# Differential attention in another order: scores one map at a time, the map turned two units later, the heads scaled by ScalarE

## What is computed

```python
def diff_attention(q, k, v, lam):
    ...
    def block(qblk):
        s = jnp.einsum('bqhcd,bkhcd->bhcqk', qblk, k).astype(jnp.float32) * scale
        pr = jax.nn.softmax(s, axis=-1)
        a = (pr[:, :, 0] - lam * pr[:, :, 1]).astype(v.dtype)
        return jnp.einsum('bhqk,bkhe->bqhe', a, v)
```

## Time and profile before

| | |
|---|---|
| time, median of 3 runs | 1784.78 us (1784.57 to 1785.18) |
| the profiled execution's own time | 1786.67 us |
| span of its trace | 1784.5 us |
| mean granted TensorE clock | 0.969 |
| busy share of the span | PE 87%, DVE 35%, ACT 14%, POOL 14% |
| attention: first scores to last product | 279.44 to 369.37 us |

### The profile page before, as it was taken

How to read it: one execution, slowest core, us unless ns; L and a number is a source line. 1 busy time by engine, 2 the same in 40 slices (tenths; PEclk the granted TensorE clock), 3 DMA queues, 4 the chain that set the end, 5 groups by cost and what they waited for, 6 DMA issues and landing times.

```text
span 1784.5 us, 19903 instructions
## 1 busy us (share of the span) xinstructions
PE 1550.3 (87%) x6788; PEld 715.9 (40%) x6788; DVE 616.7 (35%) x1194; ACT 249.2 (14%) x497; POOL 247.2 (14%) x376
## 2 busy tenths in 40 slices
PE   4999897789999999888884799999899999898881
PEld 2445444545433333333332344545433333333330
DVE  2499645743622222122123320233622222212224
ACT  2110023621100000000002111011100000000001
POOL 0024020000112111111110001000121121121110
PEclk9899998999999999999997899999999999999996
DMA  9754233041699999999997654252899999999995
GB/s 345 262 175 174 97 140 154 25 154 45 233 415 418 419 419 420 420 420 420 421 418 288 222 196 142 95 236 75 310 418 420 417 418 419 420 420 420 419 421 225
DMA packets 118640, 534.15 MB, mean 299 GB/s; under 512 B 18185, under 2 KB 19010, under 8 KB 68138
## 3 DMA queue, kind: packets, MB, share of 16 engines
q1 hardware_dynamic: 96016, 493.46, 68.9%
q0 software_dynamic: 12032, 21.08, 3.2%
q10 hardware_dynamic: 10522, 18.64, 3.0%
HBM read 522.55 MB, written 27.33 MB: 308 GB/s over the span
## 4 chain that ended last, share of the span: by engine, by line
PE 38%; SPq 19%; DMA 15%; DVE 4%; issue 3%; ACT 2%; ACTq 0%; POOLq 0%; DVEq 0%
SPq L497 18%; PE psum_pair_B L1775 12%; DMA scratch<-w_up 8%; PE psum_pair_C L1797 7%; PE psum_pair_B L1666 4%; PE psum_pair_A L1666 4%; DMA weight_ring<-w_up 3%; PE psum_pair_C L1713 3%; PE psum_pair_D L1713 3%; DMA scratch<-modulation_rows 1%; DMA weight_ring<-w_ada 1%; PE psum_pair_C L1607 1%; PE psum_pair_D L1784 1%; PE psum_pair_D L1706 1%; DVE scratch L1351 1%
## 5 line engine op out<-in xcount | busy, mean ns | idle before, releaser
L1775 PE MATMUL psum_pair_B<-weight_ring,gates_by_token 128*64 128x512 f32 x1408 | 313.5, 594 | 25.4 <-DMA weight_ring<-w_up 21.8
L1775 PE MATMUL psum_pair_B<-scratch,gates_by_token 128*64 128x512 f32 x896 | 199.3, 593 | 11.4 <-DMA scratch<-w_up 11.4
L1351 DVE TENSOR_TENSOR scratch<-psum_pair_B,scratch 128x256 f32<-128x256 f32 x72 | 30.6, 424 | 507.5 <-ACT scratch L884 507.5
L1775 PEld LDWEIGHTS psum_pair_B<-weight_ring,gates_by_token 128*64 128x64 f32 x1408 | 112.5, 137 | 218.8 <-issue 194.2
L1797 PE MATMUL psum_pair_C<-weight_ring,scratch 128*64 128x512 f32 x704 | 160.8, 597 | 25.0 <-issue 22.6
L692 POOL DMA_INDIRECT expert_rows<-scratch,scatter_rows x72 | 73.4, 1019 | 717.7 <-DVE scratch L1363 717.7
L1666 PE MATMUL psum_pair_A<-scratch,weight_ring 128*128 128x128 f32 (+1 forms) x512 | 146.4, 444 | 4.4 <-DVE scratch L1402 2.8
L884 ACT ACTIVATE scratch<-psum_pair_B 128x256 f32<-128x256 f32 x72 | 27.6, 383 | 841.9 <-PE psum_pair_B L1775 841.9
L1666 PE MATMUL psum_pair_B<-scratch,weight_ring 128*128 128x128 f32 (+1 forms) x512 | 142.2, 436 | 0.0
L1775 PEld LDWEIGHTS psum_pair_B<-scratch,gates_by_token 128*64 128x64 f32 x896 | 74.7, 137 | 131.5 <-issue 120.2
L1445 DVE SCALAR_TENSOR_TENSOR weight_ring<-weight_ring,params 128x655 f32<-128x655 f32 x120 | 117.1, 976 | 5.0 <-DVE gates_by_token L1093 0.9
(11 more groups left out here) (357 smaller groups left out, 1478.2 us busy)
## 6 DMA issues: line engine op xcount, KB each, us to landing
weight_ring<-w_gate SPq DMA_DIRECT2D x88, 1024.0 KB, 27.2
weight_ring<-w_up SPq DMA_DIRECT2D x88, 1024.0 KB, 28.2
weight_ring<-w_down SPq DMA_DIRECT2D x88, 1024.0 KB, 28.1
weight_ring<-w_ada SPq DMA_DIRECT2D x24, 2048.0 KB, 8.7
scratch<-w_up SPq DMA_DIRECT2D x40, 1024.0 KB, 27.9
scratch<-w_down SPq DMA_DIRECT2D x40, 1024.0 KB, 27.6
scratch<-w_gate SPq DMA_DIRECT2D x40, 1024.0 KB, 26.6
weight_ring<-w_in_e SPq DMA_DIRECT2D x5, 2048.0 KB, 14.5
```

The lines of the kernel that those rows point to most:

```text
L1351: tt(HID[par], PB[B_][:, 512 * par + 256:512 * par + 512], SIL[par], ALU.mult).then_inc(sig("hidden", l), 1)
L1775: ins = mm(PB[B_][CAP * q:CAP * (q + 1), 512 * par:512 * par + 512].rearrange("p (u n) -> p u n", u=2), XGT[par][:, at:at + CAP], w[:, :, ...
```

## The change

Scores and maxima are issued one map at a time: `scores(u, c)`, `maxima(u, c)`, `exps(u, c)`. TensorE now runs `scores(i, 0)`, `turn(i-2)`, `scores(i, 1)`, `values(i-2)`. VectorE runs `maxima(i, 0)`, `mixed(i-1)`, `maxima(i, 1)`; its `heads_out` is gone. ScalarE runs `turned(i-2)`, `exps(i, 0)`, `head_squares(i-3)`, `heads_out(i-2)`, `exps(i, 1)`; `heads_out` is now an ACTIVATE with Copy and a scale by partition. Its loop has one more round, VectorE's one less. The allocation of PSUM pairs and the sizes are as before.

```diff
--- before.py
+++ after.py
@@ -975,15 +975,12 @@
             act.dma_start(out["new_cache_k"].rearrange("b l t h c d -> (b l t) (h c d)"), KC).then_inc(sig("outputs_stored"), 16)
             after(act, "v", 4)
             act.dma_start(out["new_cache_v"].rearrange("b l t h c -> (b l t) (h c)"), V[:, 4, :]).then_inc(sig("outputs_stored"), 16)
-            def exps(u):
+            def exps(u, c):
                 w = NS + PAST if UNITS[u][0] < 4 else NP
-                for c in range(2):
-                    take(act, "s", u, c)
-                    act.wait_ge(sig("max_ready"), 2 * u + c + 1)
-                    if u >= 2 and c == 0:
-                        take(act, "aT", u - 2)
-                    took(act.activation(PR[:, u % 2, c, 0:w], PB[uses[("s", u, c)][0]][:, 0:w], ACT.Exp, bias=snb[:, u % 2, c:c + 1],
-                                        scale=DH ** -0.5, accum_out=sl[:, u % 2, c:c + 1]), "s", u, c)
+                take(act, "s", u, c)
+                act.wait_ge(sig("max_ready"), 2 * u + c + 1)
+                took(act.activation(PR[:, u % 2, c, 0:w], PB[uses[("s", u, c)][0]][:, 0:w], ACT.Exp, bias=snb[:, u % 2, c:c + 1],
+                                    scale=DH ** -0.5, accum_out=sl[:, u % 2, c:c + 1]), "s", u, c)
 
             def turned(u):
                 w = NS + PAST if UNITS[u][0] < 4 else NP
@@ -992,6 +989,11 @@
                     take(act, "av", u - 2)
                 took(act.activation(AT[:, u % 2, 0:w], p[:, 0:w], ACT.Copy), "aT", u)
 
+            def heads_out(u):
+                t, h = UNITS[u]
+                p = take(act, "av", u)
+                took(act.activation(OR[:, t, h * 128:(h + 1) * 128], p[:, 0:128], ACT.Copy, scale=sr[:, u % 2, 0:1]), "av", u)
+
             def head_squares(u):
                 t, h = UNITS[u]
                 after(act, "av", u)
@@ -1000,13 +1002,17 @@
                 act.activation(SQJ[u % 2], OR[:, t, h * 128:(h + 1) * 128], ACT.Square, accum_out=oss[:, 4 * t + h:4 * t + h + 1]).then_inc(sig("head_squares"), 1)
 
             NU = len(UNITS)
-            for i in range(NU + 2):
+            for i in range(NU + 3):
+                if 2 <= i < NU + 2:
+                    turned(i - 2)
                 if i < NU:
-                    exps(i)
-                if 1 <= i <= NU:
-                    turned(i - 1)
-                if i >= 2:
-                    head_squares(i - 2)
+                    exps(i, 0)
+                if i >= 3:
+                    head_squares(i - 3)
+                if 2 <= i < NU + 2:
+                    heads_out(i - 2)
+                if i < NU:
+                    exps(i, 1)
                 if i == 8:
                     modulation_columns(0)
                 if i == 14:
@@ -1482,12 +1488,11 @@
             for name, j in [("q", 2), ("q", 3)] + [("k", j) for j in range(HC)]:
                 roped(name, j)
 
-            def maxima(u):
+            def maxima(u, c):
                 w = NS + PAST if UNITS[u][0] < 4 else NP
-                for c in range(2):
-                    p = take(dve, "s", u, c)
-                    link(dve.tensor_reduce(smx[:, u % 2, c:c + 1], p[:, 0:w], AX_X, ALU.max))
-                    ts(snb[:, u % 2, c:c + 1], smx[:, u % 2, c:c + 1], -DH ** -0.5, None, ALU.mult).then_inc(sig("max_ready"), 1)
+                p = take(dve, "s", u, c)
+                link(dve.tensor_reduce(smx[:, u % 2, c:c + 1], p[:, 0:w], AX_X, ALU.max))
+                ts(snb[:, u % 2, c:c + 1], smx[:, u % 2, c:c + 1], -DH ** -0.5, None, ALU.mult).then_inc(sig("max_ready"), 1)
 
             def mixed(u):
                 w = NS + PAST if UNITS[u][0] < 4 else NP
@@ -1499,19 +1504,14 @@
                 link(stt(sr[:, u % 2, 1:2], sl[:, u % 2, 0:1], lam_neg, sr[:, u % 2, 1:2], ALU.mult, ALU.mult))
                 stt(PR[:, u % 2, 0, 0:w], PR[:, u % 2, 1, 0:w], sr[:, u % 2, 1:2], PR[:, u % 2, 0, 0:w], ALU.mult, ALU.add).then_inc(sig("a_ready"), 1)
 
-            def heads_out(u):
-                t, h = UNITS[u]
-                p = take(dve, "av", u)
-                took(ts(OR[:, t, h * 128:(h + 1) * 128], p[:, 0:128], sr[:, u % 2, 0:1], None, ALU.mult), "av", u)
-
             NU = len(UNITS)
-            for i in range(NU + 2):
-                if 1 <= i <= NU:
+            for i in range(NU + 1):
+                if i < NU:
+                    maxima(i, 0)
+                if i >= 1:
                     mixed(i - 1)
                 if i < NU:
-                    maxima(i)
-                if i >= 2:
-                    heads_out(i - 2)
+                    maxima(i, 1)
                 if i == 18:
                     router_constant(0)
 
@@ -1915,19 +1915,16 @@
                 ins = pe.transpose(p[:, h * 128:(h + 1) * 128], kT[:, h, NS:], ident)
             filled(ins, "kout")
 
-            def scores(u):
+            def scores(u, c):
                 t, h = UNITS[u]
-                ps = [fill(pe, "s", u, c) for c in range(2)]
-                rows = [slice(DH * c, DH * (c + 1)) for c in range(2)]
-                q = [qT[rows[c], h, t * 128:(t + 1) * 128] for c in range(2)]
+                p = fill(pe, "s", u, c)
+                rows = slice(DH * c, DH * (c + 1))
+                q = qT[rows, h, t * 128:(t + 1) * 128]
                 if t < 4:
-                    for c in range(2):
-                        mm(ps[c][:, 0:NS], q[c], kT[rows[c], h, 0:NS], start=True, stop=True)
-                    for c in range(2):
-                        filled(mm(ps[c][:, NS:NS + PAST], q[c], kcT[rows[c], h, :], start=True, stop=True), "s", u, c)
+                    mm(p[:, 0:NS], q, kT[rows, h, 0:NS], start=True, stop=True)
+                    filled(mm(p[:, NS:NS + PAST], q, kcT[rows, h, :], start=True, stop=True), "s", u, c)
                 else:
-                    for c in range(2):
-                        filled(mm(ps[c][:, 0:NP], q[c], kT[rows[c], h, NS:], start=True, stop=True), "s", u, c)
+                    filled(mm(p[:, 0:NP], q, kT[rows, h, NS:], start=True, stop=True), "s", u, c)
 
             def turn(u):
                 p = fill(pe, "aT", u)
@@ -1952,9 +1949,11 @@
             NU = len(UNITS)
             for i in range(NU + 2):
                 if i < NU:
-                    scores(i)
-                if 1 <= i <= NU:
-                    turn(i - 1)
+                    scores(i, 0)
+                if i >= 2:
+                    turn(i - 2)
+                if i < NU:
+                    scores(i, 1)
                 if i >= 2:
                     values(i - 2)
             cat0 = lambda k: catU[:, k, :] if k < 4 else oT[:, k - 4, :]
```

## The result

The changed kernel takes **1843.93 us** (median of 4 runs, 1841.5 to 1845.0) against 1784.67 us for the kernel before in the same comparison (1782.33 to 1785.18, 4 runs): a ratio of **1.033**, 95% interval 1.0311 to 1.0349. It is slower by 59 us, where 7.5 us less were forecast, and the time lies far outside the range.

What follows compares the result with a forecast made beforehand. The attention was taken as bound by a chain of waits, 4.41 us per unit, with no engine full. Steady part -2.3, filling -4.6, emptying -0.9 and DMA issues +0.3 summed to -7.5: 1777.3 us, range 1774.3 to 1783.5.

Steps and rivals of the forecast that it cites:

- the filling: Attention's start, up to unit 4's scores: unit 1 waits only for exponential 0, clock stays up; -4.6 us.
- The third rival: Attention: clock falls and stays low as half the rows rest; 8.2 us per unit, 1798 to 1830 us; chance 0.10.
- the emptying: From unit 16's scores to the last product's end: 14.3 us instead of 15.2; -0.9 us, bounds -2 and +1.
- unit 4's start: Its scores start near 296.7; at 301.3, as before, if the clock falls and returns only at 296.36.
- VectorE and ScalarE stopped being the bound: Attention units: VectorE 3.3 to 3.4 us, ScalarE 2.8, below TensorE's 4.22, which takes over as the bound.
- The scaled head on ScalarE: Head scaling moved from VectorE to ScalarE: 0.3 us per unit, bounds 0.2 and 0.4.
- The round of 4.22 us: TensorE's time per attention unit: two maps at 1.22, transposes 0.57, products 1.21; bounds 4.08 and 4.56.
- the change of tiling: Step from a map's last score matmul to the next full-array matmul: 0.18 us, bounds 0.11 and 0.35.
- The first rival: TensorE empties fully at tiling switches: round 4.56 to 4.6 us, total about 1783 us; chance 0.13.
- The steady part: Twelve middle attention units, each 4.22 instead of 4.41 us: -2.3 us, bounds -4.0 and +1.8.
- The DMA issues of ScalarE: Behind i = 8 in ScalarE's queue, now followed by a turned map's copy with slack of about 1.2: +0.3 us.
- Faster at all?: Whole kernel: chance 0.70 of being faster, meaning below 1781.2 us; 0.19 the same, 0.11 slower.

Runs made afterwards that it cites:

- run 4: The changed kernel with four useless full-row matmuls behind unit 0's scores and two behind unit 1's; 1785.81 us, ratio 0.9982.
- run 10: As run 4, but the useless matmuls take 64 of the 128 rows; 1785.51 us, ratio 0.9998.
- run 1: The changed kernel with each map's score matmuls over all 128 rows, so other attention values; 1774.22 us, ratio 0.9926.
- run 11: The changed kernel with the other map's score matmuls beside each map's own, unread, only from unit 4 on; 1792.5 us, ratio 1.0039.
- run 9: The changed kernel with ten extra useless full-row matmuls once, ahead of unit 4's transposes; 1813.06 us, ratio 1.0146.
- run 3: The kernel before with only its scores issued apart, VectorE and ScalarE as before; 1847.11 us, ratio 1.0327.
- run 2: The changed kernel with both maps' scores issued by turns as before, VectorE and ScalarE as changed; 1828.82 us, ratio 1.0226.
- run 6: The changed kernel with queries zero-padded to 128 rows, values kept, one expert weight load moved behind the attention; 1775.96 us, ratio 0.9934.
- run 5: The changed kernel with the other map's score matmuls run beside each map's own in the other 64 rows, unread; 1783.86 us, ratio 0.9987.

## Why the prediction was wrong

**The cause.** Three things are shown. A wait of 3.3 us lets the clock fall (runs 4 and 10 fill the wait, and the fall is gone). Then the separated scores, over half the rows and at half speed, did not get it raised again in the changed kernel, while full rows did, in the same list (runs 1 and 11); a block of full rows did too (run 9). At the high clock the same list stays up (runs 4, 9, 10). That twice the speed means twice the work in a given time would explain this; it is argued, not shown. Before, both maps ran side by side over all rows, and the clock was back at unit 3. Not shown is the rule by which the chip decides. Four things that any such rule has to meet were not taken apart: run 3's two returns with half rows, its two falls without a long wait, run 2's long low stretch with full rows, and a first wait of about the same length that let the clock fall in runs 1 and 6 (2.28 us) and not in run 5 (2.24 us).

**The step that failed** is the filling, at "this supposes that the clock stays up". It rested on 1.1 us more of work before the wait and on a wait of 2.5 us instead of 4.19. The work was never there. Unit 0's maps still ran side by side, because nothing stands between `scores(0, 0)` and `scores(0, 1)` for i < 2:

```profile
279.76 0.66 PE L1924 MATMUL psum_pair_A<-scratch 64*128 64x512 f32 x1 [0.45 <-ACT scratch L960]
279.78 0.69 PE L1924 MATMUL psum_pair_B<-scratch 64*128 64x512 f32 x1
...
284.44 1.22 PE L1924 MATMUL psum_pair_A<-scratch 64*128 64x512 f32 x1 [3.32 <-ACT scratch L982]
285.21 1.22 PE L1924 MATMUL psum_pair_B<-scratch 64*128 64x512 f32 x1
```

(Each map's first matmul; the other three of each follow.) So the wait was 3.32 us. Its end was forecast well (284.2 against 284.44); its beginning was not. Nor would the work have been a safe ground: in runs 1 and 6 unit 0's maps do stand one behind the other and the wait is 2.28 us, and the clock still fell for a while. The forecast's sum then held no term for a clock that stays down, which cost 4.14 us in each of 12 units; only the third rival priced that.

**The third rival was right** and was given 0.10. It named the mechanism, half the array's rows resting for more than half of each round, and the point from which it decides. What spoke against it, "at half clock TensorE would be busy all the time", is where I misread: I took busy time for what the clock answers to, while the row of 300 to 340 us shows 40.00 of 40 busy at 0.50. Its own price was low in three terms: 8.55 instead of 8.2 per unit (12 times 0.35 = 4.2 us); the emptying, kept at -0.9, came at half clock as well and at +4.2 (5.1); and unit 4's start, taken as before, some 21.9 us behind unit 0, came at 26.35 (4.5). 1830 and these three make 1843.8.

The Trainium skill, TensorE: Matmul & The Clock Gate, Part 1, says that the gate is set by how busy the engine has been recently. The rows agree for the fall, behind a wait of 3.32 us. For the return they disagree if busy means the engine's busy time: at 40.00 of 40 us busy the clock stayed at 0.50.

**Point by point.**
- VectorE and ScalarE stopped being the bound: right, at full clock too (run 4: TensorE busy 75.00 of 76 us). The scaled head on ScalarE takes 0.37 (forecast 0.3, bounds 0.2 and 0.4).
- The round of 4.22 us, bounds 4.08 and 4.56: at full clock it is 4.55. The term that was mis-sized is the change of tiling. I priced it only from scores to transposes (0.18). Run 4 against run 1 shows it on both sides: one map 1.27 against 1.08 (map 0), the transposes 0.70 against 0.58 (from their start to the next scores), the products 1.31 against 1.11. The first rival's size (4.56 to 4.6) was right, but not its reason: the transposes still start at 344.59, before the last score matmul ends (344.28 + 0.38). The Trainium skill, TensorEngine Tiling (Array Packing), section Key Properties, has the switch drain the engine; these rows show a cost of some 0.14 us and no full emptying in front of the transposes.
- The steady part, -2.3 us: with 4.55 it is +1.7 at full clock. The DMA issues of ScalarE, +0.3: nothing (run 4: units 4 to 15 take 54.63 us, 12 times 4.55, with the issues among them).
- The filling, -4.6 us, if the clock stays up: right in size. In run 10 unit 4 starts 17.43 us behind unit 0, 4.4 less than before.
- The emptying, -0.9 us: half of it. In run 10 the output projection starts 14.50 us behind unit 16 (352.73 to 367.23), before 14.98.
- Faster at all? Even with the clock held up, the change is worth between nothing and 0.35% (run 4), and about nothing in run 10. The full-row version (run 6) has the forecast's 7.5 us and more.

## What to carry to other kernels

Before splitting matmuls that ran side by side in the array, ask at which clock the stretch is entered and what share of the array works in each of its parts; price the loop at both clocks, and give the slow one a real chance if a wait of some us stands ahead of it. A TensorE busy without a break is no sign that its clock is up: read the granted clock first, then the busy share. Where 64-row matmuls must run apart, padding one operand with zeros to 128 rows cost TensorE nothing here (3.99 us per unit against 4.55) and, for three operations on VectorE in its idle time, gave a kernel 0.66% faster than the one before.

## What was not expected of the hardware

- The same instructions have two lasting speeds, 4.55 and 8.55 us per unit, and one block of 10.6 us of full rows moves the kernel from one to the other (run 9).
- With zeros in half of the rows the clock was back at 1.00 from 290 on (run 6); with these rows unused it stayed at 0.50 for 145 us. The first waits differed too, 2.28 and 3.32 us.
- In run 3 the clock came back near 301, fell near 321, came back near 325 and fell near 345, in units that repeat the same list, with half rows and with no wait longer than 1.02 us in between.
- Each change between 64-row and full-row matmuls costs about 0.14 us, on the way back to 64 rows too.
- Two 64-row matmuls on different rows run side by side even when they are issued map after map, with nothing of the full array between them. All four matmuls of map 0 stand ahead of map 1's in the list, and map 1's first starts 0.02 us behind map 0's first (279.76 and 279.78). So the "strictly in order" of the kernel's description does not hold for their starts.
